# A streaming encoder step on one core: last chunk's root, routing order, the chunk loaded ahead, the opening and the closing sums

## The reference, cut to what matters

```python
# mixer, mLSTM part: for each chunk of 64 tokens and head
h = num / den[..., None]
hcent = h - mean(h); hn = hcent * rsqrt(mean(hcent * hcent) + EPS)
out = dot(mix, w_out); x = x + out
# moe(rmsnorm(x)): T = 320, 32 experts, top 4, D_FF = 1024
logits = dot(x, w_router) + b_router
top_val, top_idx = top_k(logits, 4); gates = softmax(top_val)
# for each expert e, on its tokens
gu = dot(xb, w_gate_up[e]) + b_gate_up[e]            # 1024 x 2048
g = minimum(gu[:, :1024], 7); up = clip(gu[:, 1024:], -7, 7)
out = dot((up + 1) * (g * sigmoid(1.702 * g)), w_down[e]) + b_down[e]
y = sum over the 4 experts of gates * out
y = rmsnorm(x + y, norm_final)
```

## Time and profile before

| | us |
|---|---|
| median of 3 runs | 1234.81 (1234.72 to 1234.83) |
| profiled execution | 1234.98 |
| its span, first to last instruction | 1233.3 |

### The profile page before, as it was taken

The page is one execution under the profiler, slowest core; times in us unless marked ns, Lnnn a source line. Parts: engine busy times, 40 slices in busy tenths (PEclk is TensorE's granted clock), DMA queues, the critical chain, the costliest instruction groups (busy, mean ns, idle before and its releaser), DMA issues.

```text
span 1233.3 us, 21141 instructions
## 1 busy us (share of the span) xinstructions
PE 1218.0 (99%) x7773; PEld 557.4 (45%) x7774; DVE 475.0 (39%) x918; ACT 188.6 (15%) x321; POOL 245.8 (20%) x438
## 2 busy tenths in 40 slices
PE   9999999999999999999999999999999999999997
PEld 7666666778433333333433333333343333333332
DVE  6878967435422222223322222222232222222224
ACT  4741024335301100000000000000000000000002
POOL 2077860000211111111121111111111111111100
PEclk9999999999999999999999999999999999999999
DMA  8324232895999999999999999999999999999995
GB/s 234 103 69 132 88 120 71 261 397 214 377 407 398 426 429 429 427 439 428 433 434 426 438 429 429 437 426 437 430 427 439 426 435 433 427 429 428 429 424 220
DMA packets 61189, 440.51 MB, mean 357 GB/s; under 512 B 11838, under 2 KB 40290, under 8 KB 42884
## 3 DMA queue, kind: packets, MB, share of 16 engines
q1 hardware_dynamic: 59940, 439.50, 86.3%
q10 hardware_dynamic: 1216, 0.56, 0.2%
HBM read 438.18 MB, written 1.87 MB: 357 GB/s over the span
## 4 chain that ended last, share of the span: by engine, by line
PE 71%; DMA 10%; DVE 1%; ACT 0%; issue 0%; SPq 0%; DVEq 0%; ACTq 0%
PE psum L1060 32%; PE psum L1105 16%; DMA big<-in_w_gate_up_dram 10%; PE psum L1024 7%; PE psum L1010 4%; PE psum L615 4%; PE psum L593 3%; PE psum L906 2%; PE psum L1070 1%; PE psum L1091 1%; DVE acc L2062 0%; PE psum L922 0%; ACT big L1352 0%; PE psum L935 0%; PE psum L977 0%
## 5 line engine op out<-in xcount | busy, mean ns | idle before, releaser
L1060 PE MATMUL psum<-big 128*64 128x512 f32 x2048 | 471.8, 597 | 4.0 <-DMA big<-in_w_gate_up_dram 3.7
L2012 DVE TENSOR_TENSOR acc<-acc,psum 128x512 f32<-128x512 f32 (+1 forms) x192 | 123.1, 681 | 571.5 <-PE psum L1024 569.2
L1060 PEld LDWEIGHTS psum<-big 128*64 128x64 f32 x2048 | 137.8, 136 | 305.8 <-issue 284.2
L1105 PE MATMUL psum<-big 128*64 128x512 f32 x1024 | 226.8, 595 | 0.0
L615 PE MATMUL psum<-big 128*128 128x320 f32 x576 | 161.1, 436 | 0.0
L1534 POOL COPY big<-uT 96x64 bf16 x32 | 7.4, 233 | 650.6 <-PE psum L1091 649.9
L1105 PEld LDWEIGHTS psum<-big 128*64 128x64 f32 x1024 | 70.7, 137 | 134.1 <-issue 127.9
L615 PEld LDWEIGHTS psum<-big 128*128 128x128 f32 x576 | 107.6, 190 | 47.9 <-issue 5.5
L1024 PE MATMUL psum<-big 64*128 64x512 f32 (+1 forms) x384 | 106.7, 632 | 0.0
L1401 ACT ACTIVATE big<-big 128x512 f32<-128x512 f32 x32 | 20.2, 631 | 540.3 <-DVE big L2035 540.3
L1543 POOL TENSOR_SCALAR big<-cst,big 128x128 f32<-128x128 f32 x96 | 74.8, 788 | 7.7 <-POOL big L1538 7.7
(11 more groups left out here) (296 smaller groups left out, 843.3 us busy)
## 6 DMA issues: line engine op xcount, KB each, us to landing
big<-in_w_gate_up_dram SPq DMA_DIRECT2D x40, 4096.0 KB, 24.6
big<-in_w_gate_up_dram SPq DMA_DIRECT2D x42, 2048.0 KB, 13.7
big<-in_w_down_dram SPq DMA_DIRECT2D x20, 4096.0 KB, 25.4
big<-in_w_down_dram SPq DMA_DIRECT2D x19, 2048.0 KB, 14.3
big<-in_w_in_dram SPq DMA_DIRECT2D x18, 1024.0 KB, 5.2
big<-in_w_gate_up_dram SPq DMA_DIRECT2D x12, 1024.0 KB, 9.5
big<-in_w_down_dram SPq DMA_DIRECT2D x8, 1024.0 KB, 10.6
big<-in_w_s_glu_dram SPq DMA_DIRECT2D x8, 512.0 KB, 4.3
```

The lines of the kernel that those rows point to most:

```text
L1060: mm = pe.matmul(psum[SLOT * hf:SLOT * hf + SLOT, GB + gu, :], xeT[:, 4 * (c % 2) + 2 * k + c // 2, :], hidden(big[:, base:base + FF], hf) ...
L1105: mm = pe.matmul(psum[SLOT * hf:SLOT * hf + SLOT, DB, :], hT[:, m, c, :], big[:, base:base + 512], start=False, stop=(c == DN_CHUNKS - 1 a ...
L2012: v.tensor_tensor(x, x, psum[0:n, CB + hf, :], ALU.add).then_inc(S("added"), 1)
```

## The change

Six edits in one:

- `FILL[0]`: 26 matmuls of 64 moving columns in place of 14 of 128.
- `group_root` of the last chunk is planned behind projection 35 instead of 34.
- Routing: the third tile's x is turned in two parts (six blocks of 128 columns to bank 4, two to bank 0); ScalarE copies the six to SBUF, VectorE the two; the logits are made in two parts. VectorE's order differs, `rank(2,0)` and `rank(2,1)` stand behind the logits, three fills are shorter or gone, the first expert's columns lie in three banks in another order, and the first quarter of `xeT` is made ahead of the scan.
- The chunk loaded ahead is the last of expert 7.
- At the end the first half of tile 0 is added by an identity matmul, the second by VectorE into PSUM; ScalarE squares the halves separately.
- Semaphore counts follow.

```diff
+        SPARE_OF = 2 * TURN - 1
-        XT = (2, 6, 4)
+        XT, XT_BACK = (2, 6, 4), 0
+        FRONT, BACK = range(6), range(6, DK)
+        COLUMNS = {0: (XB, 0), 2: (XB, 1), 4: (HB, 0), 1: (XB + 1, 0), 6: (HB, 1), 3: (XB + 1, 1), 5: (HB, 2), 7: (HB, 3)}
-        FILL = (14, 2, 3, 3)
+        FILL = ((26, 64), (2, P), (3, P), (3, P))
-            plan[CH_SLOT[c]] += [("chunk", c), ("group_root", c)]
+            plan[CH_SLOT[c]].append(("chunk", c))
+            plan[CH_SLOT[c] + (c == NC - 1)].append(("group_root", c))
...
-                for c in range(0 if e > 1 else 2, CHUNKS - (e == TURN - 1)):
+                for c in range(0 if e > 1 else 2, CHUNKS - (e == SPARE_OF)):
...
# TensorE
-                for _ in range(FILL[n]):
-                    pe.matmul(psum[:, 1, 0:P], busy, busy, start=True, stop=True)
+                times, columns = FILL[n]
+                for _ in range(times):
+                    pe.matmul(psum[:, 1, 0:columns], busy, busy[:, 0:columns], start=True, stop=True)
...
             rows_out(2, 3)
+            x1_turned(2, FRONT, XT[2], 11)
             pe.wait_ge(S("mask_ready"), 2)
             rank(1, 0)
             rank(1, 1).then_inc(S("ranks"), 1)
-            pe.wait_ge(S("x1_ready"), 11)
-            fill(0, 2)
-            x1_turned(2, ALL, XT[2], 12)
-            fill(1, 4)
+            x1_turned(2, BACK, XT_BACK, 12)
+            fill(1, 1)
+            pe.wait_ge(S("xm_ready"), 3)
+            logits(2, FRONT)
             pe.wait_ge(S("xT_ready"), 5)
-            logits(2, ALL).then_inc(S("logits"), 1)
-            fill(1, 1)
+            logits(2, BACK).then_inc(S("logits"), 1)
+            rank(2, 0)
+            rank(2, 1)
...
             gather_tiles((0, 1))
-            rank(2, 0)
-            rank(2, 1)
             pe.wait_ge(S("mask_ready"), 3)
             rank(2, 2).then_inc(S("ranks"), 1)
...
             pe.wait_ge(S("p_ready"), 2)
-            pe.wait_ge(S("xm_ready"), 4)
-            for k in range(4):
-                for h in range(2):
-                    s64 = slice(TS * h, TS * h + TS)
-                    mm = pe.matmul(first_columns(4 * h + k), xh[s64, k * P:(k + 1) * P], one2[s64, :],
-                                   start=False, stop=True, skip_group_check=True)
+            pe.wait_ge(S("xm_ready"), 5)
+            for k in COLUMNS:
+                h, kk = k // 4, k % 4
+                s64 = slice(TS * h, TS * h + TS)
+                mm = pe.matmul(first_columns(k), xh[s64, kk * P:(kk + 1) * P], one2[s64, :],
+                               start=False, stop=True, skip_group_check=True)
+                if k == 2:
+                    mm.then_inc(S("ranks"), 1)
             mm.then_inc(S("gathered"), 1)
-            fill(1, 3)
...
             blocks = pe.value_load(cum[0:1, NE:NE + 1], min_val=1, max_val=NE * MAXB)
+            pe.wait_ge(S("added"), 6 * blocks + 2)
+            pe.matmul(psum[:, LAST[0], :], ident, acc[:, 0, 0:512], start=True, stop=False, skip_group_check=True)
             pe.wait_ge(S("osb_ready"), blocks + 1)
# ScalarE
             do(nc.scalar.activation(st[s64, 16:17], st[s64, 15:16], ACT.Identity, bias=st[s64, 14:15], scale=1.0 / D))
+            act.wait_ge(S("xmT"), 3)
+            act.wait_ge(S("logits"), 2)
+            nc.scalar.copy(xT2[:, 0:6, :], cut(psum[:, XT[2], :], DK, TS)[:, 0:6, :]).then_inc(S("xm_ready"), 1)
             act.wait_ge(S("x1_ready"), 12)
...
             for i, (t0, n) in enumerate(TILES):
+                if i == 0:
+                    act.wait_ge(S("sums"), 1)
+                    nc.scalar.activation(square2[:, 0, 0:512], psum[:, LAST[0], :], ACT.Square, accum_out=st[:, 0:1]).then_inc(S("ss"), 1)
+                    act.wait_ge(S("ss"), 9)
+                    do(nc.scalar.activation(st[:, 14:15], st[:, 0:1], ACT.Identity, bias=st[:, 13:14], scale=1.0 / D))
+                    act.wait_ge(S("acc_ready"), 1)
+                    nc.scalar.activation(square2[:, 0, 512:D], psum[:, LAST[0] + 1, :], ACT.Square, accum_out=st[:, 15:16]).then_inc(S("ss"), 1)
+                    act.wait_ge(S("ss"), 10)
+                    nc.scalar.activation(st[:, 6:7], st[:, 15:16], ACT.Sqrt, bias=st[:, 14:15], scale=1.0 / D).then_inc(S("rms"), 1)
+                    continue
# VectorE
             last_rest(0)
+            inverse(1)
             residual(2, 0)
             turned_rows(1, ALL, XT[1], 2)
-            inverse(1)
+            first_rest(1)
             residual(2, 1)
-            first_rest(1)
+            last_rest(1)
             choose(1)
+            residual(2, 2)
+            residual(2, 3)
             rank_table(0)
-            residual(2, 2)
+            turned_rows(2, BACK, XT_BACK, 4)
             one_hot(0)
-            residual(2, 3)
             rank_table(1)
             one_hot(1)
             dve.sem_inc(S("p_ready"), 1)
-            turned_rows(2, ALL, XT[2], 3)
             inverse(2)
-            last_rest(1)
             choose(2)
             rank_table(2)
             one_hot(2)
...
-            do(v.tensor_tensor_scan(cumf[:, 2, 1:], ones[0:1, 0:NE], cumf[:, (MAXB - 2) % 2, 1:], 0.0, ALU.mult, ALU.add))
-            do(v.tensor_copy(cum[:, :], cumf[:, 2, :]))
-            dve.sem_inc(S("cum_ready"), 1)
...
+            dve.wait_ge(S("ranks"), 5)
+            first_part(0).then_inc(S("xe_ready"), 1)
+            do(v.tensor_tensor_scan(cumf[:, 2, 1:], ones[0:1, 0:NE], cumf[:, (MAXB - 2) % 2, 1:], 0.0, ALU.mult, ALU.add))
+            do(v.tensor_copy(cum[:, :], cumf[:, 2, :]))
+            dve.sem_inc(S("cum_ready"), 1)
+            dve.wait_ge(S("gathered"), 2)
+            for n in range(1, 4):
+                first_part(n).then_inc(S("xe_first"), 1)
...
             for i in range(2):
                 dve.wait_ge(S("sums"), i + 1)
+                if i == 0:
+                    x = psum[:, LAST[0] + 1, :]
+                    v.tensor_tensor(x, acc[:, 0, 512:D], x, ALU.add).then_inc(S("acc_ready"), 1)
+                    continue
```

More of the change, by code:

```diff
@@ L914, in x1_turned @@
                 for k in ks:
-                    at = (k - ks[0]) * n
+                    at = k * n
                     mm = turn(psum[:, b + at // 512, at % 512:at % 512 + n], acc[0:n, i, k * P:(k + 1) * P], n)
@@ L959, in _ @@
             rank(1, 1).then_inc(S("ranks"), 1)
-            pe.wait_ge(S("x1_ready"), 11)
-            fill(0, 2)
-            x1_turned(2, ALL, XT[2], 12)
-            fill(1, 4)
+            x1_turned(2, BACK, XT_BACK, 12)
+            fill(1, 1)
+            pe.wait_ge(S("xm_ready"), 3)
+            logits(2, FRONT)
             pe.wait_ge(S("xT_ready"), 5)
-            logits(2, ALL).then_inc(S("logits"), 1)
-            fill(1, 1)
+            logits(2, BACK).then_inc(S("logits"), 1)
+            rank(2, 0)
+            rank(2, 1)
             def first_columns(k):
-                return psum[:, XB + k // 4, (k % 4) * SLOT:(k % 4 + 1) * SLOT]
+                b, at = COLUMNS[k]
+                return psum[:, b, at * SLOT:(at + 1) * SLOT]
             def gather_tiles(tiles):
                 order = [(n, q, i) for n, (q, i) in enumerate(PARTS) if i in tiles]
-                for k in range(DK):
+                for k in COLUMNS:
                     for n, q, i in order:
                         pe.matmul(first_columns(k), parts[:, i, q, k * P:(k + 1) * P], pb[:, i, :],
-                                  start=(n == 0 and k % 4 == 0), stop=(n == len(PARTS) - 1), skip_group_check=True)
+                                  start=(n == 0 and COLUMNS[k][1] == 0), stop=(n == len(PARTS) - 1), skip_group_check=True)
             pe.wait_ge(S("p_ready"), 1)
@@ L1125, in _ @@
                     s64 = slice(SLOT * hf, SLOT * hf + SLOT)
-                    mm = pe.matmul(psum[0:n, LAST[i] + hf, :], pt[s64, t0:t0 + n], osb[s64, :], start=(i < 2), stop=True,
-                                   skip_group_check=True)
+                    mm = pe.matmul(psum[0:n, LAST[i] + hf, :], pt[s64, t0:t0 + n], osb[s64, :], start=(i < 2 and i + hf > 0),
+                                   stop=True, skip_group_check=True)
                 mm.then_inc(S("sums"), 1)
@@ L1406, in experts @@
                     nc.scalar.activation(osb, psum[:, DB, :], ACT.Copy).then_inc(S("osb_ready"), 1)
-            with act.Fori(0, TURN - 1) as e:
+            with act.Fori(0, SPARE_OF) as e:
                 experts(e)
-            used = act.value_load(cum[0:1, TURN - 1:TURN], min_val=1, max_val=NE * MAXB)
+            used = act.value_load(cum[0:1, SPARE_OF:SPARE_OF + 1], min_val=1, max_val=NE * MAXB)
             act.wait_ge(S("res_landed"), 96)
@@ L1420, in _ @@
             nc.scalar.copy(big[:, at:at + last_size], big[:, last:last + last_size]).then_inc(S(half_name(TURN - 1, CHUNKS - 1)), 16)
-            with act.Fori(TURN - 1, NE) as e:
+            with act.Fori(SPARE_OF, NE) as e:
                 experts(e)
@@ L1427, in _ @@
                 else:
-                    act.wait_ge(S("acc_ready"), i + 1)
```

(21 more changed lines are left out.)

7 lines of the change are left out of this document (3 added, 4 removed).

## The result

The changed kernel takes 1237.63 us (median of 16 runs, 1235.91 to 1238.71) against 1234.8 (16 runs): ratio 1.0022, 95% interval 1.0016 to 1.0029. It is slower by 2.8 us; the forecast was 1231.9, faster by 2.9. The profiled execution took 1238.23, its span 1236.5, against 1233.3 before: +3.2 to explain.

The account below looks back on a forecast made before the run. TensorE, busy 99% of the span, was taken to bound the kernel, with six expert passes stretched by DMA. Opening +2.45, root -1.27, routing -1.9, spare chunk -1.8, tail -0.4 sum to -2.9 us: 1231.9, range 1228.7 to 1234.8.

Parts of the forecast that it names:

- Opening: TensorE's fill before the first transpose: 52 instructions paced by weight loads, 2.4 GHz from 7.06 us; +2.45 us.
- the gains: Root, routing, spare chunk and tail, the terms that make the kernel faster: 5.4 us together.
- Rival B: Opening: 2.4 GHz comes only as the projections begin; +6.5 us against gains of 5.4, 1235.9 us; chance 0.08.
- Rival A: Opening: fill duration follows moving columns, weight loads don't pace it; opening costs -0.2, total -5.6, 1229.2 us; chance 0.20.
- Root: Last chunk's root: projection 35's drain comes first, so TensorE's hole before projection 37 goes; -1.27 us.
- Routing: From the last rows_out projections to the expert loop: the loop starts sooner and the gain passes in full; -1.9 us.
- Rival C: Routing gives 0.3 rather than 1.9 us: ScalarE ends late or DMA's start isn't moved; 1233.5 us; chance 0.12.
- Spare chunk: Chunk loaded ahead: DMA queues no longer run dry at expert 3, stalls start two passes later; -1.8 us.
- Tail: After the last down matmul: identity matmul hidden, VectorE adds one half, ScalarE squares halves separately; -0.4 us.

Follow-up runs that it names:

- j2: Changed kernel with a fill of 26 matmuls of 128 moving columns instead of 64: 1232.06 us, ratio 0.9981 to the kernel before.
- h1: Control: changed kernel with one TensorE register operation at the end of an expert replaced one for one: 1237.06 us, ratio 1.0020 to the kernel before.
- h3: Changed kernel with 14 fill matmuls of 64 moving columns: 1231.93 us, ratio 0.9978 to the kernel before.
- j3: Changed kernel with the old fill (14 x 128) and VectorE's two waits for ScalarE's third-tile parts moved behind the first expert's adds: 1231.47 us.
- h2: Changed kernel with the old fill, 14 matmuls of 128 moving columns: 1230.18 us, ratio 0.9963 to the kernel before.
- i3: Changed kernel with the old fill (14 x 128) and the spare chunk again that of expert 3: 1231.74 us, ratio 0.9977 to the kernel before.
- h4: Changed kernel with its 26 fill matmuls of 64 moving columns on a stationary tile of 64 columns: 1230.14 us, ratio 0.9962 to the kernel before.
- g1: Changed kernel with the old fill (14 x 128) and TensorE's loop end loaded with bounds: 1240.51 us, 1229.58 to 1250.84 over 12 runs.

## Why the prediction was wrong, step by step

- **Opening, the step that failed.** "So the fill instructions stay 0.213 apart until 7.06, the 28th starts there, and 24 more at 0.112 end at 9.8." I took the time of the rise from a fill of 128 columns and kept it for 64. The spacing was right, the load paces the fill; but the clock didn't rise with it, and all 52 instructions, the 17 transposes and the ten fill instructions between and behind them ran (but for the last few) at the low level: +7.65, not +2.45. j2, where the columns stay 128, is the kernel that I had worked out: 1232.06 against my 1231.9. That this is so near is partly luck: its opening costs +1.40 (first projection at 13.62), as its rise is earlier than 7.06, and the gains are smaller than forecast too.
- **Rival B was right in mechanism, and low in chance and size.** It had the fill end at 12.4 (12.3 measured) and +6.5. What it undersized is what follows: +1.3 for the transposes and fills, where from the first transpose to the first projection it is 7.56 us instead of 5.03, +2.5 (in h1, which rose sooner, +1.7). Its "against" was "the array is fed without a break", which the two equal windows above show to be worth nothing; h3 has the same 3.84 of 4.00 us and rises at 11.18.
- **Rival A was wrong**: 0.214 us apart with 64 columns. By its side stood the rule of the Trainium skill (TensorE: Matmul & The Clock Gate, LDWEIGHTS), a load of columns/1.2 ns with no term for the clock. The rows disagree: 128 columns take 333 ns at the low level and 186 at the high one, 64 take 227 and 138.
- Identical fills of 128 columns rose at 4.39 (j3), 5.35 (h2) and 7.06 (before). The Trainium skill (TensorE: Matmul & The Clock Gate, Part 1: The HAM clock gate) says that the warm-up differs between runs of one kernel, and these rows agree. h2 and h3 run as many instructions, by the profile for as long (busy for 3.84 of the 4.00 us from 1.00), and rise at 5.35 and 11.18. The same section of the Trainium skill puts the warm-up down to how long TensorE has been busy rather than to a number of matmuls; with the profile's busy time, these rows disagree.
- **Root**: -1.26 in the trace, +1.45 when undone. Right.
- **Routing**: -1.9 forecast; -1.78 to the loop's start, of which the first pass gives 0.48 back. I hadn't foreseen it: ScalarE's part of the third tile now ends later against the loop, and VectorE's adds wait for it; without that wait (j3) the first pass is 0.31 shorter. Rival C is refuted: +1.49 when undone.
- **Spare chunk**: -1.8 forecast, -1.2 in the traces, 1.4 over all runs, +1.56 by medians. Mechanism and place right (221 GB/s gone, 246 back in i3), a little too large. I took it near the loss by bytes, 1.95, and the one by share of the queues, 1.4, was nearer; the stalls begin one pass later and not two, as forecast.
- **Tail**: -0.4 forecast, -0.57 and -0.59 in traces, +1.12 by medians when undone, of which about 0.5 stays unexplained.
- The gains together: 5.4 forecast, 4.6 measured (h2).

## What to carry to other kernels

A filler that keeps TensorE running may still not bring it to 2.4 GHz: here weight loads with few moving columns between them looked as busy in every column of the profile as those with twice as many. Read the level from the spacing of equal matmuls, and where a change touches what TensorE does before its first real work, give "the clock does not come" the chance that an untried filler deserves, with its price: here 7 us against parts of 1 to 2. The fills that worked here were 14 of 128 x 128 and 26 of 64 x 64; who wants a shorter or finer one changes the number, or both sides of the tile.

## What the runs showed of the hardware

- The granted clock's column prints 1.00 before the first record of the trace, in stretches whose spacing is that of 1.2 GHz.
- f32 loads depend on the clock: 186/333 ns for 128 columns, 138/227 for 64; the pace of load and matmul at the low level is 0.214 us for 128 stationary columns, with 64 moving columns as with 128, and 0.107 for 64 with 64 (h4).
- Identical fills rise at different times: 26 of 128 x 64 at 15.83, 16.33 and 18.09, 14 of 128 x 128 anywhere from 4.14 to 7.06.
- A few register instructions more in the body of TensorE's long loop (g1): 47 instruction packets instead of 21 and 13.4 us of waits for no engine or transfer, and times that differ from run to run (1229.6 to 1250.8). That it waits for its own instructions to be read again is argued from the packets, not shown.
